# First modulation in row pieces of 128 by 2048 on four groups of output partitions, with the norm's sums and root ahead of it

## The reference

```
mod = silu(cond) @ mod_w[i] + mod_b[i]            # cond: (1024,), mod_w[i]: (1024, 6144)
sh1, sc1, g1, sh2, sc2, g2 = split(mod, 6)
h = rmsnorm(x, norm_w[i, 0]) * (1 + sc1) + sh1    # rmsnorm: x * rsqrt(mean(x*x) + eps) * w
y = mixer(h)                                      # layer 0: h @ dn_w_in comes first
x = x + g1 * y
h = rmsnorm(x, norm_w[i, 1]) * (1 + sc2) + sh2
x = x + g2 * swiglu(h)
```

## Time and profile before

| | |
|---|---|
| time, median of 3 runs | 3294.92 us (3293.69 to 3295.84) |
| profiled execution | 3295.94 us, span 3294.2 us |
| mean granted TensorE clock | 0.858 |
| busy share of PE, DVE, ACT, POOL | 85%, 41%, 27%, 31% |
| read from HBM, written | 310.69 MB, 50.60 MB |
| mean DMA rate over the span | 110 GB/s |

### The profile page before, as it was taken

How to read it: one execution, slowest core, us unless ns; L and a number is a source line. 1 busy time by engine, 2 the same in 40 slices (tenths; PEclk the granted TensorE clock), 3 DMA queues, 4 the chain that set the end, 5 groups by cost and what they waited for, 6 DMA issues and landing times.

```text
span 3294.2 us, 44660 instructions
## 1 busy us (share of the span) xinstructions
PE 2803.7 (85%) x17169; PEld 2519.2 (76%) x17169; DVE 1341.8 (41%) x1868; ACT 898.7 (27%) x1333; POOL 1031.4 (31%) x357
## 2 busy tenths in 40 slices
PE   7599978888888888679999997966699999999993
PEld 3399967777777777579999996965688877787882
DVE  0400055475465466423111213344255554445554
ACT  0200123232222322202101102002255455454543
POOL 1255220221121022234646643631123222223222
PEclk9799876785786686689999998987599999999997
DMA  8333631011011011011212211211366566665665
GB/s 294 99 112 124 277 130 57 18 57 41 19 54 41 25 48 54 27 51 51 80 55 76 91 56 46 69 51 38 109 201 194 184 211 200 201 202 186 198 190 176
DMA packets 446079, 362.05 MB, mean 110 GB/s; under 512 B 13953, under 2 KB 398986, under 8 KB 446026
## 3 DMA queue, kind: packets, MB, share of 16 engines
q1 hardware_dynamic: 427946, 320.70, 30.9%
q10 hardware_dynamic: 15200, 30.15, 2.5%
q0 software_dynamic: 2880, 10.49, 0.8%
HBM read 310.69 MB, written 50.60 MB: 110 GB/s over the span
## 4 chain that ended last, share of the span: by engine, by line
PE 57%; DVE 15%; ACT 5%; issue 5%; DMA 1%; ACTq 0%; POOL 0%; DVEq 0%; POOLq 0%; SPq 0%
PE psum L585 22%; PE psum L803 8%; PE psum L569 8%; PE psum L785 3%; DVE m_prod L1633 3%; DVE m_lo L424 2%; PE psum L722 2%; PE psum L739 2%; PE psum L714 2%; PE psum L729 2%; PE psum L633 1%; PE psum L787 1%; PE psum L745 1%; DVE cy L1307 1%; DVE gu L1628 1%
## 5 line engine op out<-in xcount | busy, mean ns | idle before, releaser
L785 PE MATMUL psum<-he,m_hi 128*128 128x384 f32 x1584 | 485.4, 377 | 67.4 <-DVE m_lo L424 66.2
L424 POOL TENSOR_TENSOR m_lo<-m_raw,m_hi 128x2048 fp32r<-128x2048 f32 (+1 forms) x55 | 251.5, 4572 | 724.7 <-ACT m_hi L1122 724.7
L465 POOL TENSOR_TENSOR w_hi<-raw,zero 128x2048 fp32r<-128x2048 f32 (+2 forms) x68 | 249.2, 3664 | 683.5 <-PE psum L585 583.8
L585 PE MATMUL psum<-a_hi,w_hi 128*128 128x320 f32 x1728 | 401.1, 314 | 63.6 <-DVE a_lo L1209 32.6
L787 PE MATMUL psum<-he,m_lo 128*128 128x192 f32 x1584 | 409.0, 258 | 0.0
L585 PE MATMUL psum<-a_lo,w_hi 128*128 128x320 f32 x1728 | 397.6, 312 | 0.0
L585 PE MATMUL psum<-a_hi,w_lo 128*128 128x320 f32 x1728 | 397.3, 311 | 0.0
L501 POOL TENSOR_TENSOR ml<-lt,level 128x640 f32<-128x640 f32 x80 | 125.1, 1570 | 793.8 <-PE psum L569 793.4
L785 PEld LDWEIGHTS psum<-he,m_hi 128*128 128x128 f32 x1584 | 313.8, 198 | 76.5 <-issue 74.3
L585 PEld LDWEIGHTS psum<-a_hi,w_hi 128*128 128x128 f32 x1728 | 291.9, 190 | 72.5 <-issue 41.1
L468 POOL TENSOR_TENSOR w_lo<-raw,w_hi 128x2048 fp32r<-128x2048 f32 (+2 forms) x68 | 329.0, 4839 | 5.3
(11 more groups left out here) (287 smaller groups left out, 4562.5 us busy)
## 6 DMA issues: line engine op xcount, KB each, us to landing
m_raw<-in_moe_w_dram SPq DMA_DIRECT2D x276, 512.0 KB, 4.5
raw<-in_mod_w_dram SPq DMA_DIRECT2D x48, 512.0 KB, 3.9
raw<-in_ffn_w_dram SPq DMA_DIRECT2D x44, 512.0 KB, 4.6
mod_raw<-in_mod_w_dram SPq DMA_DIRECT2D x16, 1024.0 KB, 5.3
raw<-in_dn_w_in_dram SPq DMA_DIRECT2D x32, 512.0 KB, 4.3
m_raw<-in_moe_w_dram SPq DMA_DIRECT2D x54, 256.0 KB, 2.8
raw<-in_sc_w_in_dram SPq DMA_DIRECT2D x24, 512.0 KB, 4.2
rows_in<-raw SPq DMA_DIRECT2D x23, 512.0 KB, 7.3
```

The source lines that it names most:

```text
L424: eng.tensor_tensor(m_lo[q][:, 0:n], m_raw[q][:, 0:n], m_hi[q][:, 0:n].bitcast(F32), ALU.subtract)\
L465: pool.tensor_tensor(w_hi[s][:, 0:cols], raw[s][:, 0:cols], zero[:, :].broadcast_to([P, cols]), ALU.add)\
L585: mm = pe.matmul(psum[:, 4 * s + 2 * m + a, 0:HALF], w[:, k, m, :], v[:, k, a * HALF:(a + 1) * HALF], start=(k == 0 and n == 0), stop=(k = ...
L785: pe.matmul(psum[:, bank, 0:2 * CAP], wh[:, c:c + P], he[:, k, :, :].rearrange("p v c -> p (v c)"), start=(k == 0), stop=False)
```

## The change

The modulation's weights are now read by rows: a piece is 128 rows (one k) by 2048 columns, 1 MB in runs of 8 KB, and there are still 24 pieces in six slots. For each piece PE issues four matmuls of 512 columns, which write to output partitions 0, 32, 64 and 96 (two partitions at each) with an explicit tile position; the sums of the eight k stand in PSUM banks 0 to 2 until the last piece. Nothing is copied out between pieces. Afterwards ACT makes four copies of 2 partitions by 1536, and PE makes 12 transposes of 128 by 128 into banks 3 to 5 from a `mod_row` that DVE has cleared beforehand. DVE adds the bias in three instructions.

The sums and the root of the first norm come ahead of the modulation on PE and ACT, and the modulation waits for the root (`rms`), as both use PSUM banks 0 and 1. On DVE the adds and the reciprocal come ahead of `modulation(0)`, which is called between the reciprocal and the scaling.

```diff
-            def mod_unit(i, s):
-                dst = m_slot[s][:, 0:KT * 256].rearrange("p (k m) -> p k m", k=KT)
-                src = mod_w[0].rearrange("(k p) m -> p k m", p=P)[:, :, bass.ds(i * (N_SLOT * 256) + s * 256, 256)]
-                sp.dma_start(dst, src).then_inc(sem(f"mod_in{s}"), 16)
...
+            def mod_piece(n):
+                k, b = divmod(n, 3)
+                sp.dma_start(m_slot[n % N_SLOT][:, 0:2 * D], mod_w[0, k * P:(k + 1) * P, b * 2 * D:(b + 1) * 2 * D])\
+                    .then_inc(sem(f"mod_in{n % N_SLOT}"), 16)
+
+            for n in range(N_MOD):
+                if n >= N_SLOT:
+                    sp.wait_ge(sem("mod_used"), n - N_SLOT + 1)
+                mod_piece(n)
...
             def modulation():
 
                 pe.wait_ge(sem("cond"), 2)
-                pe.wait_ge(sem("x_evac"), TT)
...
+                pe.wait_ge(sem("rms"), 1)
+                for n in range(N_MOD):
+                    k, b = divmod(n, 3)
+                    pe.wait_ge(sem(f"mod_in{n % N_SLOT}"), 16 * (n // N_SLOT + 1))
+                    for g in range(4):
+                        mm = pe.matmul(psum[32 * g:32 * g + 2, b, :], cond[:, k, :],
+                                       m_slot[n % N_SLOT][:, 512 * g:512 * g + 512], start=(k == 0), stop=(k == KT - 1),
+                                       tile_position=(0, 32 * g))
+                    mm.then_inc(sem("mod_used"), 1)
+                pe.wait_ge(sem("mod_row"), 5)
+                for b in range(3):
+                    for c in range(4):
+                        mm = pe.transpose(psum[:, 3 + b, c * P:(c + 1) * P],
+                                          mod_row[:, b * 512 + c * P:b * 512 + (c + 1) * P], ident)
                 mm.then_inc(sem("mod_turned"), 1)
...
+            norm(0)
             modulation()
-            pe.wait_ge(sem("mod_evac"), 1)
-            norm(0)
-            pe.wait_ge(sem("rms"), 1)
+            pe.wait_ge(sem("mod_evac"), 3)
             square_units(8, U_DN_IN, a_hi, a_lo, after=0)
...
             norm(0, "x_evac", TT)
+            act.wait_ge(sem("mod_row"), 1)
+            act.wait_ge(sem("mod_used"), N_MOD)
+            for g in range(4):
+                act.activation(mod_row[32 * g:32 * g + 2, :].rearrange("q (b c) -> q b c", b=3),
+                               psum[32 * g:32 * g + 2, 0:3, :], ACT.Copy).then_inc(sem("mod_row"), 1)
             act.wait_ge(sem("alpha"), 2)
             norm_hi(0, 0)
...
-            modulation(0)
-            norm(0, a_of(0))
+            dve.memset(mod_row[:, :], 0.0).then_inc(sem("mod_row"), 1)
+            norm(0, a_of(0), between=lambda: modulation(0))
```

More of the change, by code:

```diff
@@ L196, in build @@
             sb("raw_kept", [P, 2 * UNIT], F32, turned)
-            mod_row = sb("mod_row", [P, 2 * N_MOD * P], F32, turned)
+            mod_row = sb("mod_row", [P, 3 * 512], F32, turned)
         with ExitStack() as moe:
@@ L1037, in _ @@
             act.activation(wrt_hi[:, :, :], wrt[:, :, :], ACT.Copy).then_inc(sem("small_hi"), 1)
[L1039 to L1048, removed]
-            norm(0, "x_evac", TT)
+            norm(0, "x_evac", TT)
+            act.wait_ge(sem("mod_row"), 1)
[3 more added lines that the diff above has]
+                               psum[32 * g:32 * g + 2, 0:3, :], ACT.Copy).then_inc(sem("mod_row"), 1)
             act.wait_ge(sem("alpha"), 2)
@@ L1184, in _, with norm @@
         def _(dve):
-            def norm(q, w_of, out=None):
+            def norm(q, w_of, out=None, between=None):
                 for k in range(1, KT):
@@ L1194, in norm @@
                 dve.wait_ge(sem("rstd"), q + 1)
+                if between is not None:
+                    between()
                 n = q % 2
@@ L1225, in modulation @@
             def modulation(layer):
-                bank, c0 = (6, 0) if layer == 0 else (7, MOD_COL)
                 if layer == 0:
@@ L1233, in modulation @@
                 b = col2[:, C_MODB + 48 * layer:C_MODB + 48 * layer + 48].unsqueeze(2).broadcast_to([P, 48, 2])
-                dve.tensor_tensor(mod[:, :, :], psum[:, bank, c0:c0 + 96].rearrange("p (m w) -> p m w", w=2), b, ALU.add)\
-                    .then_inc(sem("mod_evac"), 1)
-                dve.wait_ge(sem("mod_evac"), layer + 1)
+                if layer == 0:
+                    for q in range(3):
+                        dve.tensor_tensor(mod[:, 16 * q:16 * q + 16, :].rearrange("p (g c) w -> p g c w", g=4),
+                                          psum[:, 3 + q, :].rearrange("p (c g w) -> p g c w", c=4, g=4)[:, :, :, 0:2],
+                                          b[:, 16 * q:16 * q + 16, :].rearrange("p (g c) w -> p g c w", g=4), ALU.add)\
+                            .then_inc(sem("mod_evac"), 1)
+                else:
+                    dve.tensor_tensor(mod[:, :, :], psum[:, 7, MOD_COL:MOD_COL + 96].rearrange("p (m w) -> p m w", w=2),
+                                      b, ALU.add).then_inc(sem("mod_evac"), 1)
+                dve.wait_ge(sem("mod_evac"), layer + 3)
                 for n in range(2):
```

## The result

The changed kernel takes 3272.8 us (median of 4 runs, 3267.68 to 3273.56) against 3294.31 for the kernel before (4 runs, 3291.98 to 3295.84): a ratio of 0.9932, 95% interval 0.9915 to 0.9949. The profiled execution took 3272.9 us, its span 3271.1; before it was 3295.94 and 3294.2.

What follows compares the result with a forecast made beforehand. PE bound the first modulation, then the norm held the path. Unit 0 at T0 (102.2) + 41.9 = 144.1 against 169.67, 25.5 us earlier, gave 3270.4 us profiled, 3269.4 median; own range 3263 to 3277, whole range 3252 to 3285.

Steps and rivals of the forecast that it cites:

- Norm ahead: Before the modulation: memset, adds, sums and root come first, so it starts at 39.8 instead of 28.0, 11.8 us lost.
- T0: End of the transposes that follow the modulation; claimed at 102.2 us instead of 114.76.
- unit 0: First projection unit, done when ACT starts to evacuate it; claimed at 144.1 us against 169.67, 25.5 us earlier.
- Column groups: In the modulation: a piece's four matmuls run together, 0.86 us a piece at 2.4 GHz, 1.7 at 1.2 GHz.
- Weights: In the modulation: DMA is the bound, 2.65 us a piece at 396 GB/s, PE ending at 93.4.
- Rival B: Modulation's weight reads: the queue stays at 306 GB/s, 13.2 us worse, 3282.6 us; chance 0.13.
- Turning: Behind the last piece: four ACT copies take 6.0 us and twelve transposes 2.8, giving T0 at 102.2.
- Behind T0: After T0: POOL's splits hold up DVE's pieces of h; slice 1 done at T0 + 18.4, h at T0 + 32.1.
- From h to the first evacuation: From the last slice of h to unit 0's end: stays at 9.8 us, so unit 0 ends at T0 + 41.9.
- The rest: Behind unit 0: same work in the same order, with 2.2 us allowed for shifts of the clock.

Runs made afterwards that it cites:

- e7: Changed kernel with the modulation's sums in other PSUM banks, not waiting for the root, and the norm's sums behind the seventh piece; profiled time 3248.02 us.
- e4: Changed kernel reading 1024 of each piece's 2048 columns, each half used by two matmuls, values not the reference's; profiled time 3256.42 us.
- e11: The kernel before, executed once more with no edit; profiled time 3297.64 us.
- e1: Changed kernel with row pieces and column groups alone, the norm left behind the modulation; 3272.2 us, ratio 0.9927 to the kernel before.
- e2: Kernel before with only the norm moved ahead, weights still in slabs of 256 columns; ratio 0.9995 to the kernel before.
- e5: Changed kernel with POOL's split of the second unit waiting until h is complete; profiled time 3259.00 us.
- e6: Changed kernel with the turned rows in the tokens' buffer, so POOL's first split need not wait for T0; profiled time 3271.04 us.
- e8: Changed kernel with the edits of e5, e6 and e7 together; 3241.71 us, ratio 0.9851 to the kernel before.

## Why the prediction was right

It said 3269.4 us, and 3272.8 came, inside the forecast's own range. By its steps:

- **Norm ahead: right.** Memset 1.34 us (1.33 said), adds over at 36.5 (36.4), first piece at 40.01 (39.8). Its 11.8 us at the start are the wait that e7 takes away: 11.8 us at T0, 10.3 at unit 0.
- **Column groups: right.** Four pieces in a row took 3.61 us, 0.9 us each where 0.86 was said at 2.4 GHz. A piece by itself takes 1.04 us, and 1.89 (the last) where 1.7 was said at 1.2, as the end of its last records comes on top. Little hangs on it, since DMA is slower (e4). Line 714 had shown it for two groups; it holds for four.
- **Weights: right, rate mis-sized.** The first refill was used at 46.93 (46.6 said). Then 407 GB/s instead of 396, and 427 over the 24 us with a full queue, where the prediction's bound had nothing faster than about 400; PE ended at 92.43 instead of 93.4. Rival B's 306 was indeed PE's pace. The Trainium skill, "DMA: Bandwidth & Descriptors", Specifications, gives about 358 GB/s as the limit of HBM for one core; the 407 over 45 us lie above it.
- **Turning: right.** Copies 5.84 us (6.0), transposes 2.82 (2.8), T0 101.27 (102.2).
- **Behind T0: right in mechanism.** The four pieces of h end at T0 + 17.6 (slice 1 at T0 + 18.4 said); h is complete at 132.55, T0 + 31.3 (32.1).
- **From h to the first evacuation: mis-sized.** "Stays" at 9.8 us was wrong; it took 8.3. The row of before is the clock, as a row of e11, the same kernel, shows:
```profile
159.90:169.67 9.77, 9.77 (x60) 9.77 (x60) 0.01 (x1) 0.00 (x0) 0.00 (x0) 0.86 0.01 2
```
```profile
159.97:168.25 8.28, 8.28 (x58) 8.23 (x58) 0.00 (x1) 0.00 (x0) 0.00 (x0) 1.00 0.01 2
```
The same work ran at 0.86 in the one execution and at 1.00 in the other and in the changed kernel (132.60 to 141.00 above). So the 9.8 belonged to the execution, not to the kernel, and a second profile of before would have shown it. With 0.9 us from T0 and 0.8 from h these 1.5 make the 3.3 us by which unit 0 was early (140.84 against 144.1).
- **The rest: mis-sized.** Allowed were 2.2 us, and the profile gave back 5.8. The two errors have opposite signs and leave 2.5 us: 3272.9 instead of 3270.4. That the total came so close is in part luck, then; the steps up to unit 0 came as said, each within 1.5 us. "After that PE is continuously busy", by which the sum moves the end with the mark, isn't so everywhere either: from 356.8 to 421.7 us PE is busy for 40.65 of 64.9 us. A repeat of each kernel halves the difference of the rests (3130.6 against 3127.9 on the mean of two), so 2 to 6 us is the noise that the allowance should have been.

What the prediction didn't say, though its own numbers held it: the moved norm is worth almost nothing by itself. It counted 13.0 us won behind T0 (54.9 to 41.9) and 11.8 lost at the start, and e1 and e2 measured the difference at 1 us or less.

## What to carry to other kernels

Where a stationary operand is a few columns wide, spread independent matmuls over groups of output partitions, then ask at once what the next bound is: here DMA, 2.6 us a piece against PE's 0.9 to 1.0. From then on what keeps PE from freeing the first buffers is paid in full (11.8 us of T0 in e7), so work moved ahead of such a stage belongs between its pieces, not in front (e7). And when work is taken off the path, look at what its time used to cover: POOL's splits had lain beside the norm, and held up its successor on DVE until they were moved too (e5, e6, e8). A stage that one profile shows at a lower clock needs a second profile before its length goes into a sum.

## What the runs showed of the hardware

- Reads with rows of 8 KB ran at 401 to 407 GB/s over 45 and 53 us, beside matmuls, and at 427 over 24 us with a full queue; the best of the rows of before is 396 over 4 us.
- Four matmuls of 512 columns and two stationary columns, at a granted clock of 1.00, came every 0.9 us on four groups of output partitions (1.04 us from first start to last end) and every 3.43 us on one group.
- Four instructions of DVE with both tensors in SBUF took 1.94 us with POOL idle, and 6.15, 9.47 and 13.74 us as more of POOL's two-tensor instructions lay beside them.
- Two executions of one program held the low clock in one stage for 54.6 and 64.9 us, and two of another ran the same stage in 8.3 us at 1.00 and in 9.8 us at 0.86.
